# Other banks for the merge tiles, another home for T4 in the first feed-forward group, and one more opening slice on TensorE

## The reference

```python
mod = silu(c) @ ada_w + ada_b                 # six vectors: sh1, sc1, gt1, sh2, sc2, gt2
h = rmsnorm(x, pre_mix_g) * (1 + sc1) + sh1
q_r, k_r, v_r, g_r, q_s, k_s, v_s, a_r, a_s = split(h @ w_in)
ret = silu(g_r) * groupnorm(retention(q_r, k_r, v_r, pos))   # 8 heads, chunks of 64
sb = stick_breaking(q_s, k_s, v_s)                           # 8 heads, strictly causal
mixed = sigmoid(a_r) * (ret @ w_ret) + sigmoid(a_s) * (sb @ w_sb)
x2 = x + gt1 * rmsnorm(mixed @ w_out, post_mix_g)
h2 = rmsnorm(x2, pre_ffn_g) * (1 + sc2) + sh2
out = x2 + gt2 * rmsnorm(square(relu(h2 @ w_ff1)) @ w_ff2, post_ffn_g)
```

## Time and profile before

| | |
|---|---|
| profiled execution | 1781.77 us, span 1780.0 us, mean granted TensorE clock 0.992 |
| median of three runs | 1782.74 us |
| PE busy | 1725.7 us, 97% of the span |
| DVE, ACT, POOL busy | 905.0, 562.3 and 600.1 us |
| HBM traffic | 75 GB/s over the span |

### The profile page before, as it was taken

The page is one execution under the profiler, slowest core; times in us unless marked ns, Lnnn a source line. Parts: engine busy times, 40 slices in busy tenths (PEclk is TensorE's granted clock), DMA queues, the critical chain, the costliest instruction groups (busy, mean ns, idle before and its releaser), DMA issues.

```text
span 1780.0 us, 24859 instructions
## 1 busy us (share of the span) xinstructions
PE 1725.7 (97%) x9680; PEld 1432.4 (80%) x9680; DVE 905.0 (51%) x1284; ACT 562.3 (32%) x949; POOL 600.1 (34%) x256
## 2 busy tenths in 40 slices
PE   3999999999999999999999999899999999999997
PEld 3877877777989898978888998788888888888876
DVE  6756566686537374642112367645352617262526
ACT  4555565301012211111002166323333333323242
POOL 2012011242513132332334732643535353544320
PEclk8999999999999999999999999999999999999999
DMA  9001012065401010103111455111111112020212
GB/s 358 1 24 49 1 36 72 2 225 211 169 25 51 24 52 24 51 24 142 48 47 47 161 171 189 36 60 48 47 47 47 59 35 70 24 77 18 71 73 117
DMA packets 38157, 135.13 MB, mean 76 GB/s; under 512 B 5940, under 2 KB 6836, under 8 KB 37560
## 3 DMA queue, kind: packets, MB, share of 16 engines
q1 hardware_dynamic: 30240, 109.66, 18.3%
q10 hardware_dynamic: 7832, 24.28, 3.7%
HBM read 121.33 MB, written 12.60 MB: 75 GB/s over the span
## 4 chain that ended last, share of the span: by engine, by line
PE 91%; DVE 4%; DMA 2%; POOL 1%; issue 1%; ACT 1%; SPq 1%; POOLq 0%; DVEq 0%; ACTq 0%
PE ps L533 16%; PE ps L531 16%; PE ps L532 16%; PE ps L903 5%; PE ps L905 5%; PE ps L904 5%; PE ps L610 3%; PE ps L611 3%; PE ps L612 3%; PE ps L643 2%; PE ps L660 2%; PE ps L627 2%; PE ps L783 2%; PE ps L785 2%; PE ps L784 2%; DMA ada_s<-ada 1%
## 5 line engine op out<-in xcount | busy, mean ns | idle before, releaser
L438 POOL TENSOR_TENSOR w_hi<-raw,zero 128x1024 fp32r<-128x1024 f32 x58 | 113.2, 1952 | 473.4 <-PE ps L533 272.1
L533 PE MATMUL ps<-r_hi,w_lo 128*128 128x512 f32 x640 | 254.3, 397 | 0.0
L531 PE MATMUL ps<-r_hi,w_hi 128*128 128x512 f32 x640 | 251.5, 393 | 2.1 <-issue 2.1
L532 PE MATMUL ps<-r_lo,w_hi 128*128 128x512 f32 x640 | 252.8, 395 | 0.0
L531 PE MATMUL ps<-w_hi,a_hi 128*128 128x256 f32 x768 | 219.2, 285 | 1.4 <-DVE a_lo L1619 0.6
L533 PE MATMUL ps<-w_hi,a_lo 128*128 128x256 f32 x768 | 215.5, 281 | 0.0
L532 PE MATMUL ps<-w_lo,a_hi 128*128 128x256 f32 x768 | 215.3, 280 | 0.0
L472 POOL TENSOR_TENSOR w_lo<-w,w_hi 128x1024 fp32r<-128x1024 f32 x39 | 99.9, 2561 | 221.4 <-ACT w_hi L1219 221.4
L1711 DVE TENSOR_TENSOR m<-m,ps 128x512 f32<-128x512 f32 x208 | 136.4, 684 | 71.2 <-PE ps L905 70.7
L903 PE MATMUL ps<-w_hi,f_hi 128*128 128x512 f32 x392 | 156.0, 398 | 4.9 <-issue 3.8
L904 PE MATMUL ps<-w_lo,f_hi 128*128 128x512 f32 x392 | 156.1, 398 | 0.0
(11 more groups left out here) (232 smaller groups left out, 3445.7 us busy)
## 6 DMA issues: line engine op xcount, KB each, us to landing
raw<-wstream SPq DMA_DIRECT2D x112, 512.0 KB, 3.5
ada_r<-ada_rows SPq DMA_DIRECT2D x32, 512.0 KB, 4.8
w<-wstream SPq DMA_DIRECT2D x32, 512.0 KB, 3.5
ada_s<-ada SPq DMA_DIRECT2D x7, 1024.0 KB, 17.4
m_dram<-m1s ACTq DMA_DIRECT2D x1, 4096.0 KB, 14.7
m<-m_dram ACTq DMA_DIRECT2D x1, 4096.0 KB, 12.2
x_dram<-m ACTq DMA_DIRECT2D x8, 512.0 KB, 4.0
rl_f<-x_dram ACTq DMA_DIRECT2D x2, 2048.0 KB, 10.2
```

Source lines behind the costliest of these rows:

```text
L438: nc.gpsimd.tensor_tensor(w_hi[:, slot, part], raw[:, h, :], zero[:, 0:1].broadcast_to([P, RAW]), ALU.add).then_inc(w_split, 1)
L531: nc.tensor.matmul(outp, lh, rh, start=(k == 0), stop=False)
L532: nc.tensor.matmul(outp, lh, rl, start=False, stop=False)
L533: last = nc.tensor.matmul(outp, ll, rh, start=False, stop=(k == chunks - 1))
```

## The change

ADA_PE gets slice 15: PE multiplies it after the sum of the second vector, and DVE's chain is one slice shorter, 13 in all. 20 transposes into bank 1, whose result nobody reads, stand between slice 10 and that sum, and 12 more behind slice 15. POOL makes the low parts of weight piece 1 only when scale1 and shift1 are there.

The merge's gate tiles go to banks 6, 7, 0, 1 and its branch tiles to 4, 5, 2, 3. The first gate piece's first two tiles wait for no bank, nor do the first branch piece's. The first output piece waits for gate tiles in banks 0 and 1 and for branch tiles in banks 2 and 3.

In the first feed-forward group t4 lies in y's last row (t4_first), for which POOL waits until that row is normalised and written out. DVE's s2 no longer waits for P4's low weight part, and the P1 evictions come before the low part of P6. ACT scales chunks 8 to 11 before the first hidden tile's eviction and 12 to 15 before the fourth's, and issues the three loads of the second gate's rows there.

```diff
-ADA_PE = (2, 10)
+ADA_PE = (2, 10, 15)
+        t4_first = y[:, T - 1, :]
+        def gate_bank(j):
+            return ps[:, (6, 7, 0, 1)[j], :]
+        def branch_bank(j):
+            return ps[:, (4, 5, 2, 3)[j], :]
...
                     pool.wait_ge(stick_whi, 2 * n + h + 1)
+                    if n == 1 and h == 0:
+                        pool.wait_ge(ada_ev, 2)
...
-                add(t4, t2, b21, ALU.subtract).then_inc(ff_t, 1)
+                if first:
+                    pool.wait_ge(n2_x, T)
+                    pool.wait_ge(x2_out, 16 * T)
+                add(t4_first if first else t4, t2, b21, ALU.subtract).then_inc(ff_t, 1)
                 add(b12, b22, b12, ALU.subtract).then_inc(ff_t, 1)
-                low(g, 4 + P4, 1, t4)
+                low(g, 4 + P4, 1, t4_first if first else t4)
...
-                pe.wait_ge(ada_sum, 7 if v == 0 else 14)
+                pe.wait_ge(ada_sum, 7 if v == 0 else 13)
...
+            def keep_busy(n):
+                for q in range(n):
+                    nc.tensor.transpose(ps[:, 1, q % 4 * P:(q % 4 + 1) * P], x_slot(q % 4)[:, 0:P], id_f[:, :])
             ada_summed(0)
             ada_slice(10)
-            ada_summed(1).then_inc(ada_mm, 1)
+            keep_busy(20)
+            ada_summed(1)
+            ada_slice(15).then_inc(ada_mm, 1)
+            keep_busy(12)
...
-            piece_T(PC_MERGE, 0, a_hi, a_lo, lambda j: (ev_dve, EV_MERGE - 3 + j), after=last_r)
+            piece_T(PC_MERGE, 0, a_hi, a_lo, lambda j: None if j < 2 else (ev_dve, EV_MERGE - 5 + j), bank=gate_bank, after=last_r)
             pe.wait_ge(r_lo_done, 4 * RET_G)
-            piece_T(PC_MERGE + 1, 1, r_hi, r_lo, lambda j: None, banks=px)
+            piece_T(PC_MERGE + 1, 1, r_hi, r_lo, lambda j: None if j < 2 else (ev_dve, EV_MERGE - 3 + j), bank=branch_bank)
...
-                        lambda t: (ev_act, EA_MERGE + 4 * MERGE_G - 3 + t) if p == 0 else (ev_act, EA_OUT + 4 * p + t % 4 - 3),
+                        lambda t: (ev_act, EA_OUT + 4 * p + t % 4 - 3) if p else (ev_act, EA_MERGE + 4 * MERGE_G - 1 + t) if t < 2
+                        else (ev_dve, EV_MERGE + 4 * MERGE_G - 3 + t),
...
-            for u in range(8, 16):
-                scale_h2(u)
...
                 for j in range(4):
+                    if first and j in (0, 3):
+                        for u in range(8, 12) if j == 0 else range(12, 16):
+                            scale_h2(u)
+                    if first and j == 3:
+                        rows2_loads()
                     hidden(g, order, j)
...
-                dve.wait_ge(ff_wlo, FF_UNITS * g + 4 + P4 + 1)
+                if not first:
+                    dve.wait_ge(ff_wlo, FF_UNITS * g + 4 + P4 + 1)
                 dve.wait_ge(ff_s, 4 * g + 1)
                 V.tensor_tensor(s2, a22, a21, ALU.subtract).then_inc(ff_s, 1)
                 f_low(P4, a22)
+                if first:
+                    dve.wait_ge(x2_out, 16 * T)
+                    for t in range(4):
+                        evict(P1, t, px[:, t, :], 0, 0, ALU.add, ev)
                 f_low(P6, s2)
                 V.tensor_tensor(a11, s2, a11, ALU.add).then_inc(ff_s, 1)
-                if first:
-                    dve.wait_ge(x2_out, 16 * T)
-                for t in range(4):
-                    evict(P1, t, px[:, t, :], 0, 0, ALU.add, ev)
+                if not first:
+                    for t in range(4):
+                        evict(P1, t, px[:, t, :], 0, 0, ALU.add, ev)
```

More of the change, by code:

```diff
@@ L534, in tile, with piece_T @@
                 last.then_inc(sem, 1)
-            def piece_T(n, slot, xh, xl, free, banks=pg, chunks=KC, cols=256, order=TT, after=None):
+            def piece_T(n, slot, xh, xl, free, bank=lambda j: pg[:, j % 4, :], chunks=KC, cols=256, order=TT, after=None):
                 pe.wait_ge(w_split, 4 * n + 4)
@@ L541, in piece_T @@
                         pe.wait_ge(*free(j))
-                    tile(banks[:, j % 4, :],
+                    tile(bank(j),
                          lambda k: tuple(w[:, slot, k * cols + m * P:k * cols + (m + 1) * P] for w in (w_hi, w_lo)),
@@ L834, in last_r @@
                     r_transposed(RET_G - 1, u)
-            piece_T(PC_MERGE, 0, a_hi, a_lo, lambda j: (ev_dve, EV_MERGE - 3 + j), after=last_r)
+            piece_T(PC_MERGE, 0, a_hi, a_lo, lambda j: None if j < 2 else (ev_dve, EV_MERGE - 5 + j), bank=gate_bank, after=last_r)
             pe.wait_ge(r_lo_done, 4 * RET_G)
-            piece_T(PC_MERGE + 1, 1, r_hi, r_lo, lambda j: None, banks=px)
+            piece_T(PC_MERGE + 1, 1, r_hi, r_lo, lambda j: None if j < 2 else (ev_dve, EV_MERGE - 3 + j), bank=branch_bank)
             with pe.Fori(1, MERGE_G) as g:
-                piece_T(PC_MERGE + 2 * g, 0, a_hi, a_lo, lambda j: (ev_act, EA_MERGE + 4 * g - 3 + j))
-                piece_T(PC_MERGE + 2 * g + 1, 1, r_hi, r_lo, lambda j: (ev_dve, EV_MERGE + 4 * g - 3 + j), banks=px)
+                piece_T(PC_MERGE + 2 * g, 0, a_hi, a_lo, lambda j: (ev_act, EA_MERGE + 4 * g - 3 + j), bank=gate_bank)
+                piece_T(PC_MERGE + 2 * g + 1, 1, r_hi, r_lo, lambda j: (ev_dve, EV_MERGE + 4 * g - 3 + j), bank=branch_bank)
             def h2_transposed(u):
@@ L1124, in _ @@
                     act.wait_ge(gl_mm, 4 * g + j + 1)
-                    nc.scalar.activation(gate[:, j % 2, :], pg[:, j, :], ACT.Sigmoid).then_inc(ev_act, 1)
+                    nc.scalar.activation(gate[:, j % 2, :], gate_bank(j), ACT.Sigmoid).then_inc(ev_act, 1)
             act.wait_ge(gemm_done, TL_MERGE + MERGE_TILES * (MERGE_G - 1) + 4)
@@ L1207, in _, with rows2_loads @@
             square_x2(7)
-            for u in range(8, 16):
-                scale_h2(u)
-            act.dma_start(gtg2[:, :], mods[3:4, :].broadcast_to([P, D])).then_inc(rows2_in, 16)
-            act.dma_start(adab2, adab[5:6, :].broadcast_to([P, D])).then_inc(rows2_in, 16)
-            act.dma_start(postg2, postg[1:2, :].broadcast_to([P, D])).then_inc(rows2_in, 16)
+            def rows2_loads():
+                act.dma_start(gtg2[:, :], mods[3:4, :].broadcast_to([P, D])).then_inc(rows2_in, 16)
+                act.dma_start(adab2, adab[5:6, :].broadcast_to([P, D])).then_inc(rows2_in, 16)
+                act.dma_start(postg2, postg[1:2, :].broadcast_to([P, D])).then_inc(rows2_in, 16)
             def w_high(slot, src, free, *ready):
@@ L1267, in ff_group @@
                     hidden(g, order, 7)
-                    w_second(P4, t4, ff_t, 4 * g + 3)
+                    w_second(P4, t4_first, ff_t, 4 * g + 3)
                 f_high(P4, a22, ff_sq, 8 * g + (8 if first else 7))
@@ L1608, in merge @@
                     dve.wait_ge(ev_act, EA_MERGE + 4 * g + j + 1)
-                    V.tensor_tensor(gate[:, j % 2, :], px[:, j, :], gate[:, j % 2, :], ALU.mult).then_inc(ev_dve, 1)
+                    V.tensor_tensor(gate[:, j % 2, :], branch_bank(j), gate[:, j % 2, :], ALU.mult).then_inc(ev_dve, 1)
                     dve.wait_ge(ev_dve, EV_MERGE + 4 * g + j + 1)
```

## The result

The changed kernel takes 1767.51 us (median of 6, 1766.56 to 1772.27) against 1782.11 (median of 6): ratio 0.992, interval 0.9909 to 0.9931, 14.6 us less. Forecast were 14.0 us less. A later set gave 1768.53 (5 executions) against 1783.09, 14.6 again.

The account below looks back on a forecast made before the run. TensorE, holding 91% of the chain of waits, was taken to bound the kernel. Opening -2.0, merge -4.1 and first feed-forward group -7.9 sum to -14.0 us: 1767.8 profiled, 1768.7 as median, range 1765.5 to 1773.5.

Parts of the forecast that it names:

- columns of 3.5 us: Opening: sign of being wrong; the forecast wanted the sum's 16 column instructions near 1.84 us in the profile after.
- rival A: Opening: clock stays at 1.2 GHz through the columns; first matmul 2.0 us late, +2.0 not -2.0, 1772.7 us; 20%.
- Steps 1 and 2: Opening: sum starts 1.0 us earlier behind 20 transposes; columns then run at full clock, ending at 39.2, 0.6 us won.
- step 4: Opening: first big matmul starts 1.1 us earlier; of the 1.7 us slow stretch 0.7 is left, 1.0 won.
- The normalised rows on DVE: Opening: rows of the second half expected to be late next on DVE, costed at 0.1 us.
- (a): First feed-forward group: earlier eviction of the first hidden tile ends PE's wait for its bank, -2.1 us, at worst -1.7.
- (b): First feed-forward group: with t4 in y's last row the stop before P4 shrinks from 3.76 to about 0.7, -3.1 us.
- (c): First feed-forward group: eight matmuls at 0.427 us after the stop before P4 go with it, -1.6 us, bound 0.
- (d): First feed-forward group: the 1.1 us stop on L1706 goes, the f_lo chain some 8 us ahead; -1.1, at worst 0.
- Rivals B: First feed-forward group: order on shared POOL and DVE work stays bad, stop of 3.1 again; 4.0 less gain, 1772.7; 10%.
- C: Merge: start held by something other than its bank (weights, r parts); 4.1 us less gain, 1772.8; 3%.
- D: Opening leaves the clock low well beyond 47 us; slower, 1786.7 us with 40 us more of it; 3%.

Follow-up runs that it names:

- e1: The opening part of the change alone on the kernel before: 1780.98 us, ratio 0.9989.
- e9: The changed kernel itself timed once more, nothing altered: 1768.53 us, median of five executions.
- e7: The changed kernel without POOL's wait for scale1 and shift1 (ada_ev): 1769.59 us.
- e12: The changed kernel, transposes kept, with ACT making the second half of weight piece 2's high part at once: 1765.51 us, ratio 0.9902.
- e5: The changed kernel with the opening of before, so merge and feed-forward parts together: 1768.59 us, ratio 0.9922.
- e2: The merge part of the change (other banks) alone on the kernel before: 1778.58 us, ratio 0.9977.
- e3: The feed-forward part of the change alone on the kernel before: 1773.20 us, ratio 0.9946.
- e10: The kernel before with only the new order of ACT's scalings and first hidden evictions: 1779.80 us, ratio 0.9983.
- e11: e3 with the P1 evictions back at their old place, behind f_lo of P6 and a11: 1779.44 us, ratio 0.9979.
- e6: The changed kernel without its 20 and 12 transposes, slice 15 still on PE and POOL's wait kept: 1770.83 us.
- e4: The changed kernel with 10 and 6 matmuls of 512 columns in place of the 20 and 12 transposes: 1767.55 us, ratio 0.9915.
- e8: e4 with ACT also making the second half of weight piece 2's high part at once: 1764.96 us, ratio 0.9907.

## Why the prediction was right

The time came out as forecast, and merge and feed-forward came out by the steps given. The opening did not, and the prediction's own sign of being wrong, columns of 3.5 us, stood in the profile after. That the total fits all the same is in part luck.

**Opening.** -2.0 was forecast. What it brings depends on where the clock rises and falls between 30 and 48 us, and the forecast summed one course of it (with 20% for another, rival A). The profiles show three. ACT's place against the kernel before at 95 us tells what each leaves; the six profiles with the old opening scatter there from -0.5 to +0.5.
- No rise in the 20 transposes (after, e1, e9): +0.6 to +0.8. This is rival A's course: columns of 3.4 and 3.6 us, DVE 2.2 us late, the first big matmul 1.7 us late (forecast 2.0). Rival A's price of 2.0 was too high, since it left the slow stretch as before: the first big matmul starts nearer to the rise at 46.7, and five run slowly instead of eight.
- A rise, and a low stretch behind it that lasts into the big matmuls (e7, without POOL's wait): -0.1. Steps 1 and 2 hold, and step 4 fails: it gave the slow stretch 1.0 less, and it grew from eight big matmuls to ten.
- A rise, and the next one before the second big matmul (e12): -3.6 at 57 us and -2.9 at 95. The columns end at 38.4 (forecast 39.2), the first big matmul starts at 41.34 (42.0), and the whole slow stretch of 1.7 us is won, not 1.0. The normalised rows on DVE, costed at 0.1, then stop PE for 0.5 us at 54.

By the times the opening is worth 1.1 us alone (e1, interval 0.4 to 3.6) and 0 to 1.1 on top of the rest (e5). So it is the mis-sized term: the forecast put 2.0 on it as the usual course, and two of the three courses seen give nothing or take a little. What decides between the courses was not tested.

The sentence of the Trainium skill ("TensorE: Matmul & The Clock Gate", Part 4: PE-mode transpose) that the full clock doesn't engage for transposes would have made rival A the rule. Three of the five profiles with the 20 transposes look like that; e7 and e12 show the clock rising among them, and where page and measurement differ, the measurement decides.

**Merge.** -4.1 was forecast, 4.5 less measured in the profile and 4.4 less in e2's. Alone it gave 3.5; a fall behind a later stop took 1.5 back in e2's profile, and in the full change that later stop is gone.

**Feed-forward.** -7.9 was forecast, 8.3 measured in the profile, 8.9 by e3. (a) exact at 2.1 in the profile; e10 gives 3.3 by its median, and that the 1.2 above come from falls behind the stop is argued from e2. (b) the stop fell from 3.76 to 0.39, 3.4 for 3.1. (c) no slow stretch behind it, as forecast. (d) the stop on L1706 is gone, but my reason gave the reordered evictions no price of their own; e11 gives it: 5.2 us of the part's 8.9 hang on their place.

**The sum** came out 0.6 us short of the measured 14.6, by two errors that cancel: the opening 0.9 to 1.9 too high, merge and feed-forward together 2.2 too low against e5's 14.2. I priced the falls of one execution only; e2 and e10 hint that a stop I took at its bare 2.1 us costs 1.2 to 1.5 more in others. That this makes up the 2.2 is argued, not shown. e5's own profile has only part of it: by the matching its merge gives 4.5 and its feed-forward group 8.1, 12.7 together for the forecast 12.0. Of its 13.5 us in all, 0.5 lie in the opening, which it has as before, and 0.4 in the output projection; the other 1.0 of its 14.5 against its set is that the kernel before was profiled in an execution 1.0 below that set's median. Two products are rounded up in the prediction, 6 x 0.19 to 1.2 and 8 x 0.19 to 1.6; that is 0.1 in all. The range held all eleven executions of the changed kernel. Rivals B, C and D did not come.

## What to carry to other kernels

Price a stop of the bounding engine at its length plus what its clock may lose behind it, and remove the small ones too: one of 1.4 us cost 1.4 in most profiles and 2.9 in two. Where gpsimd and VectorE both work from SBUF, put VectorE's instructions that read PSUM beside gpsimd and its SBUF-only ones into gpsimd's gaps; the order alone was worth 5 us here (e3 against e11). Filling a stop of PE so as to hold its clock up is no gain by itself: work and warming about cancelled here (e5, e6). A part whose effect hangs on the clock needs several executions before one profile is believed: both profiles of the changed kernel showed the opening as a loss of 0.6 to 0.8 us, while in e12 it gained 2.9.

## What the runs showed of the hardware

The same stop drew a clock fall in one execution and not in another. The 1.4 us stop on POOL's low part near 100 us stands in twelve profiles and has granted 0.50 behind it in two (the first profile after and e1; 1.00 in the kernel before and in e9). The 2.1 us stop at the fifth hidden tile stands in three and has it in one (e2). The stops of 2.95 to 3.76 us at the merge and in the feed-forward group have it in all ten cases (kernel before, e1, e2, e3, e10, e11). Such a fall cost 1.5 us (after at 101 us, e2 at 1103).

The clock rose in the last microsecond of the 20 transposes in e7 and e12, and not in the two profiles of the changed kernel or in e1, with the same instructions, started within 0.5 us of one another. The 16 one-column matmuls did not hold it: it fell during slice 15's in e4, e7, e8 and e12, between 36.5 and 38.5 us, though it had risen at 33 to 35. With the old opening, the same instructions on PE each time, it rose for the big matmuls anywhere from 46.6 (e5) to 48.8 us (e3).
